# Block two of a three-block network: earlier norms, more choosing steps in phase one, ScalarE scales the maps, TensorE adds the position table

## The reference, cut to what matters

```python
# end of block one: output projection, residual, norm; then block two's own input norm
h = layer_norm(ALPHA * h + mix, ln_g, ln_b)
h = layer_norm_2(x, ln_in_g, ln_in_b)
# block two
proj = x @ w_in + b_in                    # 1024 -> 3912 columns, split in 16 parts
yb = chunk_band_attention(...)            # 4 heads, window of up to 5 tiles, relative bias
yc = dsa_attention(...)                   # 4 heads, keys chosen by an index score
ym = memory_attention(...)                # 4 heads, 256 memory tokens
mixed = concat([ya*silu(a_g), yb*silu(bg), yc*silu(cg), ym*silu(mg)]); y = mixed @ w_out + b_out
# inside dsa_attention, for each query row:
score = einsum('bqhs,bqh->bqs', relu(logits), iwb * 8 ** -0.5)   # 8 index heads
_, idx = lax.top_k(score, 256)                                   # the 256 best keys
s = q . k[idx] * dh ** -0.5 + t5_table[bucket(idx - qpos)]       # position table
p = softmax(s); out = p @ v[idx]
```

## Time and profile before

| | us |
|---|---|
| median of 3 runs | 3742.96 (3741.97 to 3743.91) |
| the profiled execution: its own time | 3743.01 |
| its span | 3741.1 |
| busy in the span: PE / DVE / ACT / POOL | 3158.5 / 2121.0 / 1150.9 / 395.3 |
| mean granted TensorE clock | 0.924 |

### The profile page before, as it was taken

How to read it: one execution, slowest core, us unless ns; L and a number is a source line. 1 busy time by engine, 2 the same in 40 slices (tenths; PEclk the granted TensorE clock), 3 DMA queues, 4 the chain that set the end, 5 groups by cost and what they waited for, 6 DMA issues and landing times.

```text
span 3741.1 us, 37549 instructions
## 1 busy us (share of the span) xinstructions
PE 3158.5 (84%) x14208; PEld 2411.4 (64%) x14208; DVE 2121.0 (57%) x3233; ACT 1150.9 (31%) x2184; POOL 395.3 (11%) x383
## 2 busy tenths in 40 slices
PE   6999889886888799499987731689986989999999
PEld 5787667665777687377875531344454468888887
DVE  5013444586788636538777699466875334444444
ACT  2212221785666622134214420100156111111111
POOL 2000012342111101121430000001000000000000
PEclk9999989996999999799998875899988999999999
DMA  5322135335433153142452500411110111111111
GB/s 210 131 82 88 45 122 174 130 113 161 98 96 99 44 200 127 42 100 66 131 173 79 173 8 0 152 61 49 46 46 9 51 34 45 55 48 45 45 46 68
DMA packets 189934, 326.63 MB, mean 87 GB/s; under 512 B 16242, under 2 KB 110610, under 8 KB 189754
## 3 DMA queue, kind: packets, MB, share of 16 engines
q1 hardware_dynamic: 168602, 250.29, 21.7%
q0 software_dynamic: 21152, 73.94, 5.5%
HBM read 233.71 MB, written 89.16 MB: 86 GB/s over the span
## 4 chain that ended last, share of the span: by engine, by line
issue 50%; PE 25%; DVE 14%; ACT 5%; POOL 3%; DMA 3%; SPq 1%; DVEq 0%; ACTq 0%; POOLq 0%
PE banks L215 7%; PE banks L2111 6%; PE banks L1546 4%; PE banks L508 3%; DVE b2late_sel L2299 3%; PE banks L184 2%; DVE b2late_top L2297 2%; ACT b1att_map L1370 2%; PE banks L206 1%; DVE b1att_map L1397 1%; ACT b1scan_R L987 1%; DVE b1att_map L1419 1%; DVE b2maps_map L2645 1%; SPq L128 1%; ACT b2turn_turned L2573 1%
## 5 line engine op out<-in xcount | busy, mean ns | idle before, releaser
L215 PE MATMUL banks<-b3h4a_hi,b3mlpw_part 128*128 128x512 f32 x1024 | 318.9, 390 | 6.8 <-DVE b3mlpw_part L3239 6.8
L215 PE MATMUL banks<-b3mlpw_part,b3mlp_acthi 128*128 128x512 f32 x1024 | 315.2, 389 | 0.0
L215 PE MATMUL banks<-b1ln_w,b_hThi 128*128 128x512 f32 x768 | 239.6, 393 | 0.0
L215 PEld LDWEIGHTS banks<-b3h4a_hi,b3mlpw_part 128*128 128x128 f32 x1024 | 193.0, 189 | 47.3 <-issue 7.1
L3286 DVE TENSOR_TENSOR b3out_x<-b3out_x,banks 128x1024 f32<-128x1024 f32 x128 | 154.7, 1218 | 111.7 <-PE banks L215 111.7
L215 PEld LDWEIGHTS banks<-b3mlpw_part,b3mlp_acthi 128*128 128x128 f32 x1024 | 192.2, 188 | 39.9
L215 PE MATMUL banks<-b3out_lo,b3mlpw_part 128*128 128x512 f32 x512 | 199.9, 390 | 0.0
L215 PE MATMUL banks<-b3mlpw_part,b3mlp_actlo 128*128 128x512 f32 x512 | 199.2, 389 | 0.0
L508 PE MATMUL banks<-b_hThi,b1item_hi 128*128 128x512 f32 x464 | 196.0, 422 | 3.4 <-DVE b1item_lo L497 3.1
L206 PE MATMUL banks<-fixed_eye,b2maps_map 128*128 128x128 f32 x328 | 63.4, 313 | 157.9 <-DVE b2maps_map L2618 157.8
L2111 PE MATMUL banks<-b2h_hi,b2h_whi 128*128 128x512 f32 (+1 forms) x448 | 178.7, 399 | 15.6 <-POOL b2h_wlo L2069 10.6
(11 more groups left out here) (415 smaller groups left out, 6919.9 us busy)
## 6 DMA issues: line engine op xcount, KB each, us to landing
qk_spill<-b1scan_qk SPq DMA_DIRECT2D x64, 256.0 KB, 2.7
b1att_k<-qk_spill SPq DMA_DIRECT2D x64, 256.0 KB, 8.2
b1out_ws<-in_w_out SPq DMA_DIRECT2D x16, 1024.0 KB, 5.1
b3mlpw_stage<-in_w_mlp_up SPq DMA_DIRECT2D x16, 1024.0 KB, 5.3
b3mlpw_stage<-in_w_mlp_down SPq DMA_DIRECT2D x16, 1024.0 KB, 4.9
b2h_stage<-in_w_in SPq DMA_DIRECT2D x30, 512.0 KB, 3.9
b1item_stage<-in_w_in SPq DMA_DIRECT2D x29, 512.0 KB, 4.7
b1ln_stage<-in_w_in SPq DMA_DIRECT2D x12, 1024.0 KB, 5.6
```

Of the source, the lines that this page charges most:

```text
L215: last = pe.matmul(out, x, y, start=i == 0, stop=i == n - 1)
```

## The change

At the end of the output projection VectorE norms tiles 4 to 7 ahead of the halves that it used to wait for, items 0 and 1 are split earlier, and SyncE loads tiles 4 to 6 of `h` ahead of item 1. In phase one the credit is 1.9 per quarter throughout, less 0.4 per index score unit. In the attention the credit is 1.0 per round in all kinds; the map is scaled by ScalarE in round r + 1; the reciprocal moves to round r + 1 as well, ahead of the next shift; the position table of d is added by TensorE for tiles 2 to 7 as a first product with the identity (plain float32), so that the shift adds the chosen mask alone and L2636 goes; TensorE's order in a round is now scores, turn, values, and ScalarE's is scaling, exponential, copy. The band's queries, tables and keys are loaded 4 transfers at a time, behind the items bv 1 to dk 1. The buffer of `C.mask` becomes an unused gap of 4 KB.

```diff
 sp_out1:
-    sp_item2(K, 1)
     for st in range(4, ST):
+        if st == 7:
+            sp_item2(K, 1)
         sp.wait_ge(S["pj_h2"], st - 3)
         L.start(sp, ("b1p", "h", st), m.r[st % 4], K.h_dram[st * P:(st + 1) * P, :])
-        if st == 4:
-            sp_item2(K, 2)
-    for n in range(3, FIRST2):
+    for n in range(2, FIRST2):
         sp_item2(K, n)
 act_out1: item 0 behind group 13, item 1 behind group 15,
           item 2 behind turn 3, item 3 behind half 0, item 4 behind turn 4
 dve_out1:
+        if g == 13:
+            dve_item2(K, 0)
...
-    for n in range(2):
-        dve_item2(K, n)
+    dve_item2(K, 1)
...
     for st in range(4, ST):
         residual(st)
-    for n, kind in TAIL1:
...
+    for st in range(4):
+        low(st)
+    dve_item2(K, 2)
+    both(4); dve_half(K, 0); dve_item2(K, 3)
+    both(5); dve_half(K, 1); low(4); dve_item2(K, 4)
+    both(6); dve_half(K, 2); low(5)
+    both(7); dve_half(K, 3); low(6); dve_half(K, 4); low(7)
 sp_two:
-        if ITEMS2[n] == ("mq", 1):
+        if n == ITEM_AT[("bv", 1)]:
             ...
-            attention_queries(K, K.m_band)
-        if ITEMS2[n] == ("dq", 1):
+            attention_queries(K, K.m_band, (0, 1))
+        if n == ITEM_AT[("mq", 0)]:
+            attention_queries(K, K.m_band, (2, 3))
+        if n == ITEM_AT[("mq", 1)]:
+            attention_tables(K, K.m_band)
             for k in range(2):
                 sp.wait_ge(*K.stores[("b2y", k)])
-            attention_keys(K, K.m_band)
-            attention_tables(K, K.m_band)
+        if ITEMS2[n][0] in ("dq", "dk"):
+            attention_keys(K, K.m_band, [n - ITEM_AT[("dq", 0)]])
 dve_two:
-            top.pump(1.7 if scored == ST - 1 else 0.6, scored)
+            top.pump(1.9, scored)
...
+            top.credit -= 0.4
 pe_attend (order now scores r, turn r - 3, values r - 4):
+            chosen = A.sel and t in K.sel
+            if chosen:
+                pe.wait_ge(S["at_edge"], 4 + h + 1)
+                pairs = [(K.eye, A.bias(h, t)[:, x:x + n])] if chosen else []
+                last = products(pe, ..., pairs + [(q, k[part][:, x:x + n]) for part in range(2)])
 act_attend (scaling r - 1, exponential r, copy r - 3):
+            a.wait_ge(S["at_one"], u + 1)
+            a.activation(e, e, ACT.Copy, scale=s[:, 2:3]).then_inc(S["at_scaled"], 1)
 dve_attend:
-            top.pump({"b": 1.0, "m": 0.5, "d": 0.5}[A.kind], ST - 1)
+            top.pump(1.0, ST - 1)
-        u = r - 2
+        u = r - 1
             v.wait_ge(S["at_exp"], u + 1)
-            vs.mark(v.reciprocal(s[:, 2:3], s[:, 1:2]))
-            v.wait_ge(vs.sem, vs.n)
-            v.tensor_scalar(e, e, s[:, 2:3], None, ALU.mult).then_inc(S["at_scaled"], 1)
+            v.reciprocal(s[:, 2:3], s[:, 1:2]).then_inc(S["at_one"], 1)
...
-                vs.mark(v.tensor_tensor(C.mask[:, 0:width], bias, K.sel[t], ALU.add))
-                v.wait_ge(vs.sem, vs.n)
-                bias = C.mask[:, 0:width]
+                bias = K.sel[t]
   (the gate moves from round r + 4 to the end of round r + 5)
```

More of the change, by code:

```diff
@@ L1658, in dve_out1, with low, both @@
     v.wait_ge(vs.sem, vs.n)
+    def low(st):
+        cols = slice(st * P, (st + 1) * P)
+        v.wait_ge(S["pj_hT"], st + 1)
+        v.tensor_tensor(K.h2lo[:, :, cols], by_k(turn_pair(K, st)), K.h2hi[:, :, cols], ALU.subtract).then_inc(S["pj_hlo"], 1)
+    def both(st):
+        first(st)
+        second(st)
     for st in range(4, ST):
         residual(st)
-    for n, kind in TAIL1:
[L1662 to L1672, removed]
+    for st in range(4):
+        low(st)
+    dve_item2(K, 2)
+    both(4)
+    dve_half(K, 0)
+    dve_item2(K, 3)
+    both(5)
+    dve_half(K, 1)
+    low(4)
+    dve_item2(K, 4)
+    both(6)
+    dve_half(K, 2)
+    low(5)
+    both(7)
+    dve_half(K, 3)
+    low(6)
+    dve_half(K, 4)
+    low(7)
 def project_one_over(K, e):
@@ L2525, in pe_attend @@
     for r in range(ALL_UNITS + 4):
[L2526 to L2532, removed]
-                pe.wait_ge(S["at_gate"], T - 1)
-            pe.wait_ge(S["at_copied"], u + 1)
-            out = K.bank[4 + T % 2][(h % 2) * HD:(h % 2 + 1) * HD, (h // 2) * P:(h // 2 + 1) * P]
-            products(pe, out, [(val, C.turned[u % 3][:, i]) for i, val in enumerate(A.vals(h, t))]).then_inc(S["at_av"], 1)
-        u = r - 3
-        if 0 <= u < ALL_UNITS:
-            bank, before = C.turn_banks[u]
-            width = C.widths[u]
-            if before is not None:
-                pe.wait_ge(S["at_copied"], before + 1)
-            pe.wait_ge(S["at_scaled"], u + 1)
-            transposed(pe, bank_span(K, bank, width), [C.maps[u % 4][:, i * P:(i + 1) * P] for i in range(width // P)], K.eye).then_inc(S["at_turned"], 1)
         u = r
@@ L2559, in pe_attend @@
                 n = min(512, width - x)
-                last = products(pe, bank_span(K, bank, width)[:, x:x + n], [(q, k[part][:, x:x + n]) for part in range(2)])
+                pairs = [(K.eye, A.bias(h, t)[:, x:x + n])] if chosen else []
+                last = products(pe, bank_span(K, bank, width)[:, x:x + n], pairs + [(q, k[part][:, x:x + n]) for part in range(2)])
             last.then_inc(S["at_sc"], 1)
+        u = r - 3
+        if 0 <= u < ALL_UNITS:
+            bank, before = C.turn_banks[u]
+            width = C.widths[u]
+            if before is not None:
+                pe.wait_ge(S["at_copied"], before + 1)
+            pe.wait_ge(S["at_scaled"], u + 1)
+            transposed(pe, bank_span(K, bank, width), [C.maps[u % 4][:, i * P:(i + 1) * P] for i in range(width // P)], K.eye).then_inc(S["at_turned"], 1)
+        u = r - 4
+        if u >= 0:
+            A, h, t = stage_of(K, u)
+            T = u // 4
+            if u % A_UNITS == 0:
+                pe.wait_ge(*K.loads[(A.kind, "v")])
+            if h == 0 and T >= 2:
+                pe.wait_ge(S["at_gate"], T - 1)
+            pe.wait_ge(S["at_copied"], u + 1)
+            out = K.bank[4 + T % 2][(h % 2) * HD:(h % 2 + 1) * HD, (h // 2) * P:(h // 2 + 1) * P]
+            products(pe, out, [(val, C.turned[u % 3][:, i]) for i, val in enumerate(A.vals(h, t))]).then_inc(S["at_av"], 1)
 def act_attend(K):
@@ L2589, in dve_attend @@
                 v.wait_ge(*K.stores[("pass", n, part)])
-    for r in range(ALL_UNITS + 5):
+    rows_free()
+    for r in range(ALL_UNITS + 6):
         u = r
@@ L3433, in block_two_memory @@
     queries(a, dsa)
-    dsa.table, mask = a.take("table", [P, 4, S_LEN]), a.take("mask", [P, S_LEN])
-    mem0 = a.at
+    dsa.table = a.take("table", [P, 4, S_LEN])
+    mem0 = a.at + 4096
     a = Space(nc, "b2mem", mem0, late0)
```

78 lines of the change are left out of this document (41 added, 37 removed).

## The result

The changed kernel takes 3631.49 us (median of 4 runs, 3631.21 to 3631.85) against 3742.63 (3741.97 to 3743.91); ratio 0.9703, 95% interval 0.9686 to 0.972. Forecast: 3632. The profiled execution has a span of 3630.0 us, 111.1 less than before.

A forecast was written before the change was run, and what follows sets the result against it. Bounds taken: an engine-alternating chain in the output projection's end, TensorE in phase one, VectorE's choosing in parts of the attention. Terms -48 - 8 - 55 = -111 on span 3741.1 gave 3630.1, so 3632 us; range 3605 to 3693.

The forecast's parts named there:

- End of the output projection: Term 1, end of the output projection: VectorE's own work becomes the chain, last lower part at 1545.4 instead of 1593.3, -48 us.
- Phase one, the steps: Phase one: 13 more choosing steps, 26 us of VectorE's work, mostly in idle time; +4 us, bounds 0 and +13.
- Phase one, the transfers: Phase one: spreading the transfers removes TensorE's 9.85 us stall for weights and the half clock behind it; -12 us.
- Band and memory: Attention's band and memory stages: rounds set by a loop of shift, exponential and reciprocal; band -6 us, memory +3 us.
- d: Attention's stage d: TensorE the bound from tile 4, 77 us of choosing, tile 7 30 us; 191 against 243.2, -52 us.
- 1 (TensorE held back, +30): Stage d: added float32 products and half clock hold TensorE back; +30 us, 3662 us, chance 0.16.
- 2 (-20): Attention: shorter rounds, TensorE's added work hidden in its waits, tile 7 ending sooner; -20 us, 3612 us, chance 0.17.
- the lower bound: Attention term's bound of -75 us: TensorE's extra work hidden and tile 7 at 22 us.
- 3 (stall stays): Phase one: the 9.85 us stall stays or moves, +12 us, and VectorE is late, +9; 3653 us, chance 0.13.
- 4 (serial rounds): Attention: each round becomes one serial chain, 524 us against 405; slower kernel at 3806 us, chance 0.02.
- 5: Whole change: nothing won, choosing merely moved into a full phase one and norms still waiting for halves; 3743 us, chance 0.02.

The follow-up runs named there:

- x1: The changed kernel with only the end of the output projection as in the kernel before; 3681.1 us.
- x2: The changed kernel with only the choosing credit of phase one as before (0.6, then 1.7, nothing taken off per score unit); 3647.06 us.
- x3: The changed kernel with the band's query, key and table transfers as before, behind items mq 1 and dq 1, keys and tables in one block; 3647.0 us.
- x5: The changed kernel with reciprocal and scaling of a unit two rounds after its exponential instead of one; 3621.46 us.
- x4: The changed kernel with the position table of d added by VectorE again, not by TensorE; 3629.05 us.
- x9: The changed kernel with TensorE's order in an attention round as before (values, turn, scores), ScalarE's order staying new; 3872.18 us.
- x8: The changed kernel with 2.3 us of choosing per quarter instead of 1.9 in phase one once the last tile's scores are there; 3604.08 us.

## Why the prediction was right, step by step

- **End of the output projection**: forecast -48, measured -50.8. The order of VectorE's work was the chain, as drawn; a half took the 0.74 to 0.75 us of the estimate. Of the 2.8 us, 1.6 are block one's: tile 3 is normed at 1482.5 and not at 1484.1. Two places were drawn wrong and cancelled. The 4.8 us allowed for tile 7's load did not come, but four residuals stand there (4.62 us) and not one. The idle time before the last lower part was 0.73 us instead of 3.2, but two halves and a lower part (2.7 us), which the sum leaves out, stand between norm 7 and it. x1 prices the part at 50.
- **Phase one, the steps**: forecast +4, and x2 gives 4.9. TensorE's waits for the norm of v (ScalarE's relu) are 6.9 us, with the old credit 2.4. 121 MAX8 before the attention, 120 forecast.
- **Phase one, the transfers**: forecast -12; x3 gives 12.8. The Trainium skill's rule (Trainium Kernel Development and Optimization, Key Constraints) that queues share 16 DMA engines does not by itself decide whether there is a stall: the bytes are the same in both, and the stall comes and goes with the order on the queue. The trace of x3 agrees with the rule all the same, as the load behind the block landed in 9.5 us and the spread one in 4.4. Phase one and turn together: -4.2 measured against -8. Of the 3.8 us between them 2.1 are the turn, 15.0 against 12.9 us, where a choosing step stands that I had not costed (x2). The rest, 1.6 us between x2's and x3's prices and phase one's -6.3, is within the 2 us to which that stage repeats.
- **Band and memory**: -5.7 and +0.4, for -6 and +3. The loop of shift, exponential and reciprocal was there (42.1 us of waits at the reciprocal, 14.1 of them in the band), and x5 shows that it set the rounds; in the band TensorE's scores were the next bound, only 2.6 us away. I took 0.70 us for the scaling of 640 elements on ScalarE; it was 0.825. This had little effect, as ScalarE wasn't the bound. The Trainium skill's page ScalarE: Activation LUTs (Step-by-step: what each stage is for) has one element per cycle whatever the function; the row agrees, with exponential and scaling alike at 0.83 and 0.825. What I had missed is the part that doesn't grow with the columns (last section). The prediction's sentence on VectorE is worded too widely: the Trainium skill (VectorE: DVE Perf Modes, The perf-mode tier table) has the doubled rate for copies and for tensor_scalar, which the scaling is, and not for every float32 operation on one tensor.
- **d**: forecast -52, measured -49.7. To the last shift of tile 6 86.6 us (84 forecast), choosing 75.6 (77), tile 7 31.3 (30). From tile 4 on TensorE was full at clock 1.00.
- **Rivals.** 1 (TensorE held back, +30) is refuted: without the added products d is only 5.3 us shorter (x4), and the clock from tile 4 on was 1.00. 2 (-20) did not come: x4 shows the products hidden to all but 5 us, but VectorE and ScalarE stand close behind, and tile 7 took 31.3 us and not the 22 of the lower bound. 3 (stall stays): refuted, x3. 4 (serial rounds), which had a chance of 0.02: it did not happen, but x9 shows how near it is. With one engine's order unchanged the attention takes 595.6 us (turn, band, memory and d), the rival's sum had 524. Its "against", that each step reads data of a round that is ready, is not enough of a reason: in x9 they are ready too. What excludes the ring is the order on all three engines together, which the prediction did not go through. 5: refuted.

The mechanisms were as drawn, with the two exceptions at the end of the output projection and the turn left out. In size the terms were off by up to 4 us, with both signs: -2.8, +3.8, 0.0 for the attention (its parts +0.3, -2.6 and +2.3), and -1.1 in the rest of the kernel, which the sum held fixed. That they cancel to 0.5 us in the total is luck.

## What to carry to other kernels

When a software pipeline is reordered, write down each engine's order in a round and look for rings through them, however old the data: an old copy behind a new exponential together with new scores behind old values cost 241 us. With both engines in the new order, or both in the old one, there was no ring. Put filler work where its engine waits for another at full load, and price it there: a step of 2.5 us cost nothing beside TensorE in tiles 4 to 6 of d and about 0.6 (9.1 us for 16) in late phase one. Where an engine is about to wait for a transfer, a piece of filler work belongs ahead of the wait: behind it, one step lengthened the turn by 2.1 us (that it is free ahead of the wait was not tried). Transfers that nobody needs yet go between the urgent loads a few at a time, as a block of 20 ahead of a weight load cost a stall of 10.7 us without a byte more.

## What the runs showed of the hardware that was not expected

- ScalarE's scaling by a column, from SBUF to SBUF, takes 0.825 us for 128x640 float32, its copy from PSUM 0.684 and VectorE's scaling 0.554. Before the change only the last two were to be seen, and the copy was the wrong one to go by. The rate is the same for all three on ScalarE: from 128 to 640 columns the exponential goes from 0.402 to 0.828 us, the scaling from 0.403 to 0.825 and the copy from 0.255 to 0.684, 0.82 to 0.84 ns a column each. What differs is the fixed part, some 0.15 us less for the copy.
- A float32 product of 512 columns and the scores for them take 1.32 us together at full clock (2247.41 to 2248.73 below, TensorE in tile 7 after). The rows give the sum of the two alone. It is the 0.88 forecast from the earlier trace rows and twice 0.219, and yet taking all these products out of d saved 5.3 us: three engines had nearly the same load there.

```profile
2247.41 1.02 PE L184 MATMUL banks<-b2dsa_table,fixed_eye 128*128 128x512 f32 x2
2247.87 1.02 PE L184 MATMUL banks<-b2dsa_dk,b2dsa_dq 128*128 128x512 f32 x2
2248.73 1.03 PE L206 MATMUL banks<-fixed_eye,b2maps_map 128*128 128x128 f32 x8
```

- VectorE at 94% and TensorE at 97% of the same 180 us, with POOL's 67.09 us and DMA at 0.51 beside them (x8): four engines and the DMAs ran side by side at that load; the 16 steps, some 41 us of VectorE's work, lengthened phase one by 9.1.
